# A three-block transformer forward pass: remainders of the weights on GpSimd, halves of k in another order in three stages, and another order for the queries of cross-attention

## What is computed

```python
for i in range(2):
    h = h + 0.5 * swiglu(rms_norm(h, ffa_norm[i]), ffa_w_gate_up[i], ffa_w_down[i])
    hn = rms_norm(h, mix_norm[i])
    h = h + (even_mixer(hn, ...) if i == 0 else odd_mixer(hn, ...))
    h = h + 0.5 * swiglu(rms_norm(h, ffb_norm[i]), ffb_w_gate_up[i], ffb_w_down[i])
    gate = sigmoid(rms_norm(h, ple_norm[i]) @ ple_w_gate[i])
    h = h + gate * (p[i] @ ple_w_proj[i])
x = rms_norm(h, final_norm)
proj = rmsnorm(x, norm_mix_g) @ w_in          # q, k, v, gelu inputs, two gates
x = x + (sigmoid(gate_a) * (moba(q, k, v) @ w_a) + sigmoid(gate_b) * (gmlp(u, v) @ w_b)) @ w_out
x = x + cross_attention(rmsnorm(x, norm_xa), rmsnorm(mem, norm_mem)) 
x = x + peer(rmsnorm(x, norm_ffn))            # top 16 of 128 x 128 keys per head, 8 heads
return rmsnorm(x, final_g)
```

## Time and profile before

| | |
|---|---|
| time, median of 3 runs | 2117.62 us (2116.42 to 2120.50) |
| the profiled execution's own time | 2120.12 us |
| its span in the trace | 2118.3 us |
| TensorE busy | 2091.8 us, 10466 matmuls |
| VectorE busy | 1338.4 us |
| ScalarE busy | 1049.0 us |
| GpSimd busy | 31.2 us, 42 instructions |
| remainders on VectorE (L267) | 336, 2290 ns each |
| w_hi on ScalarE (L262) | 336, 1915 ns each |
| mean granted TensorE clock | 0.997 |

### The profile page before, as it was taken

How to read it: one execution, slowest core, us unless ns; L and a number is a source line. 1 busy time by engine, 2 the same in 40 slices (tenths; PEclk the granted TensorE clock), 3 DMA queues, 4 the chain that set the end, 5 groups by cost and what they waited for, 6 DMA issues and landing times.

```text
span 2118.3 us, 25812 instructions
## 1 busy us (share of the span) xinstructions
PE 2091.8 (99%) x10466; PEld 1744.0 (82%) x10466; DVE 1338.4 (63%) x1793; ACT 1049.0 (50%) x1262; POOL 31.2 (1%) x42
## 2 busy tenths in 40 slices
PE   9999899999999999999999999999999999999998
PEld 7888788888888888888888878888888888888887
DVE  5445765456545566554675756799888656666665
ACT  5445564446444556444657555546455544444443
POOL 0100000000000000000100000000000000000000
PEclk9999999999999999999999999999999999999999
DMA  6654335554555442555554535577799997676772
GB/s 254 215 183 177 119 133 192 196 180 180 182 196 180 177 140 105 194 183 192 186 185 160 177 119 199 179 243 238 240 270 272 281 329 310 261 268 258 268 258 109
DMA packets 96596, 433.72 MB, mean 205 GB/s; under 512 B 7680, under 2 KB 41104, under 8 KB 51936
## 3 DMA queue, kind: packets, MB, share of 16 engines
q1 hardware_dynamic: 95152, 426.50, 57.2%
q0 software_dynamic: 1328, 5.58, 0.8%
HBM read 397.45 MB, written 34.60 MB: 204 GB/s over the span
## 4 chain that ended last, share of the span: by engine, by line
PE 94%; DVE 3%; ACT 1%; issue 1%; DMA 0%; POOL 0%; SPq 0%; POOLq 0%; DVEq 0%
PE bank L300 28%; PE bank L302 28%; PE bank L301 28%; PE bank L305 5%; PE bank L2224 2%; DVE w_lo L267 1%; PE bank L907 1%; PE bank L880 1%; PE bank L2057 0%; DMA h<-in_x 0%; DVE x_lo L336 0%; DVE arena L800 0%; ACT w_hi L262 0%; ACT arena L938 0%; ACT x_hi L327 0%
## 5 line engine op out<-in xcount | busy, mean ns | idle before, releaser
L267 DVE TENSOR_TENSOR w_lo<-raw,w_hi 128x2048 fp32r<-128x2048 f32 x336 | 768.7, 2290 | 510.0 <-ACT w_hi L262 509.9
L262 ACT ACTIVATE w_hi<-raw 128x2048 fp32r<-128x2048 f32 x336 | 643.0, 1915 | 721.2 <-PE bank L302 704.7
L300 PE MATMUL bank<-w_hi,x_hi 128*128 128x512 f32 (+1 forms) x2080 | 822.0, 395 | 4.6 <-DVE x_lo L336 3.3
L302 PE MATMUL bank<-w_hi,x_lo 128*128 128x512 f32 (+1 forms) x2080 | 810.1, 389 | 0.0
L301 PE MATMUL bank<-w_lo,x_hi 128*128 128x512 f32 (+1 forms) x2080 | 809.4, 389 | 0.0
L300 PEld LDWEIGHTS bank<-w_hi,x_hi 128*128 128x128 f32 x2080 | 391.5, 188 | 84.0 <-ACT gated L408 3.1
L302 PEld LDWEIGHTS bank<-w_hi,x_lo 128*128 128x128 f32 x2080 | 391.0, 188 | 82.1
L301 PEld LDWEIGHTS bank<-w_lo,x_hi 128*128 128x128 f32 x2080 | 391.7, 188 | 76.2
L300 PE MATMUL bank<-w_hi,a_hi 128*128 128x512 f32 x624 | 246.6, 395 | 0.2 <-DVE a_lo L995 0.2
L302 PE MATMUL bank<-w_hi,a_lo 128*128 128x512 f32 x624 | 243.2, 390 | 0.0
L301 PE MATMUL bank<-w_lo,a_hi 128*128 128x512 f32 x624 | 243.0, 389 | 0.0
(11 more groups left out here) (202 smaller groups left out, 1222.8 us busy)
## 6 DMA issues: line engine op xcount, KB each, us to landing
raw<-in_w SPq DMA_DIRECT2D x338, 1024.0 KB, 4.8
parked_t<-arena SPq DMA_DIRECT2D x32, 512.0 KB, 8.9
arena<-parked_t SPq DMA_DIRECT2D x8, 2048.0 KB, 9.4
arena<-parked_a SPq DMA_DIRECT2D x32, 512.0 KB, 5.8
parked_a<-one_i SPq DMA_DIRECT2D x21, 512.0 KB, 7.3
parked_a<-mid SPq DMA_DIRECT2D x11, 512.0 KB, 7.0
raw<-in_w SPq DMA_DIRECT2D x8, 256.0 KB, 6.3
one_i<-in_alibi POOLq DMA_DIRECT2D x1, 1024.0 KB, 5.2
```

The costliest lines, as they stand in the source:

```text
L262: act.activation(w_hi[:, u % RING, :, :], raw[:, u % RING, :, :], ACT.Copy).then_inc(*act_done.mark("w_hi", u))
L267: e.tensor_tensor(w_lo[:, u % RING, :, :], raw[:, u % RING, :, :], f32(w_hi[:, u % RING, :, :]), ALU.subtract).then_inc(*dve_done.mark("w_ ...
L300: pe.matmul(out, hi, w_hi[:, s, b, 0:width], start=start, stop=False)
L302: return pe.matmul(out, lo, w_hi[:, s, b, 0:width], start=False, stop=stop)
```

## The change

**GpSimd makes the remainders.** `lent` are the units from 8 on but for the two plain ones and nine `own` ones (ffa1 + 2 to + 5, units 85 to 88, and in2 + 2 to + 6, units 172 to 176). Their w_lo are made by GpSimd in the new `remainders`, called between its roots, clears and DMA issues; VectorE's `split_lo` skips them. `take` and `load_unit` wait for the engine that makes the remainder.

```diff
+        own = {u0 + i for u0, n in ((first["ffa1"] + LEAD, 4), (first["in2"] + LEAD, 5)) for i in range(n)}
+        lent = set(range(8, N_UNITS)) - set(plain) - own
+        def remainder_made(u):
+            return (pool_done if u in lent else dve_done)["w_lo", u]
...
-                sp.wait_ge(*dve_done["w_lo", u - RING])
+                sp.wait_ge(*remainder_made(u - RING))
...
+        def split_lo(dve, u):
+            if u < N_UNITS and u not in plain and u not in lent:
...
+        def remainders(pool, u0, u1):
+            for u in range(u0, u1):
+                if u in lent:
+                    pool.wait_ge(*act_done["w_hi", u])
+                    pool.tensor_tensor(w_lo[:, u % RING, :, :], raw[:, u % RING, :, :], f32(w_hi[:, u % RING, :, :]),
+                                       ALU.subtract).then_inc(*pool_done.mark("w_lo", u))
...
-            pe.wait_ge(*dve_done["w_lo", u])
+            pe.wait_ge(*remainder_made(u))
```

```diff
+        CROSSED = ("ffa1", "od_in", "in2")
+        for n in CROSSED:
+            u = first[n]
+            stored[u + 1], stored[u + 2] = u + 2, u + 1
...
+            tensor_up_half(pe, n, 0, 0, first[n], lambda: tensor_normed(pe, n, prev, 1), ready)
+            if n in CROSSED:
+                tensor_up_half(pe, n, 1, 0, first[n] + 1)
+                tensor_up_half(pe, n, 0, 1, first[n] + 2, None, ready)
+                tensor_up_half(pe, n, 1, 1, first[n] + 3)
+                tensor_back(pe, n, 0)
```

```diff
-            scalar_normed(act, "xa", 1, "xa", prev, XA_BANKS)
-            split_hi(act, q0 + LEAD)
-
-            act.activation(small[:, 80:81], gains[:, 0:1], ACT.Exp, scale=0.0)
+            scalar_normed(act, "xa", 1, "xa", prev, XA_BANKS,
+                          lambda: act.activation(small[:, 80:81], gains[:, 0:1], ACT.Exp, scale=0.0))
             act.wait_ge(*pe_done["block", "xq", 0, 0])
             scale_out(act, 0, bank[4][:, :], qn_x[:, 0, :]).then_inc(*act_done.mark("xq"))
+            split_hi(act, q0 + LEAD)
             split_hi(act, q0 + 1 + LEAD)
```

More of the change, by code:

```diff
@@ L262, in split_hi @@
                 act.activation(w_hi[:, u % RING, :, :], raw[:, u % RING, :, :], ACT.Copy).then_inc(*act_done.mark("w_hi", u))
[L264 to L268, removed]
+        def split_lo(dve, u):
+            if u < N_UNITS and u not in plain and u not in lent:
+                dve.wait_ge(*act_done["w_hi", u])
+                dve.tensor_tensor(w_lo[:, u % RING, :, :], raw[:, u % RING, :, :], f32(w_hi[:, u % RING, :, :]),
+                                  ALU.subtract).then_inc(*dve_done.mark("w_lo", u))
+        def remainders(pool, u0, u1):
[4 more added lines that the diff above has]
+                                       ALU.subtract).then_inc(*pool_done.mark("w_lo", u))
         def load_by_chunks(sp, u, meanwhile=None):
@@ L546, in ffn_down, with tensor_up_half @@
             return first[n] + (3 * c + 6 if c < NFC - 2 else 2 * NFC + c)
[L548 to L565, removed]
-                if i == 0 and meanwhile:
-                    meanwhile()
+        def tensor_up_half(pe, key, c, i, u, between=None, ready=None, free=None):
+            s = u if u < 2 else take(pe, u)
+            for t in range(NT):
+                if free:
+                    free(t)
+                if t == 1 and between:
+                    between()
+                for k in range(UB):
+                    kk = i * UB + k
+                    if ready and t == 0:
+                        ready(kk)
+                    last = product(pe, bank[gu(c)[t]][:, :], s, k, BLK, x_hi[:, kk, t * P:(t + 1) * P],
+                                   x_lo[:, kk, t * P:(t + 1) * P], kk == 0, kk == KC - 1)
+                last.then_inc(*pe_done.mark("unit", u, t))
+                if i == 1:
+                    pe_done.also("up", key, c, t)
+            pe_done.also("used", u)
         def tensor_down_half(pe, key, c, half):
@@ L671, in vector_ffn @@
                 vector_first_rest(dve)
-            split_lo(dve, ffn_up(n, 0) + 1 + LEAD)
-            both(0)
+            split_lo(dve, first[n] + 1 + LEAD)
+            if n not in CROSSED:
+                both(0)
             for c in range(1, NFC):
                 split_lo(dve, ffn_up(n, c) + LEAD)
+                if n in CROSSED and c == 1:
+                    both(0)
                 split_lo(dve, ffn_up(n, c) + 1 + LEAD)
@@ L1311, in tensor_odd @@
             unit(0)
+            unit(2)
             unit(1)
@@ L1833, in pool_moba @@
             pool.memset(values_m, 0.0).then_inc(*pool_done.mark("cleared", "moba"))
+            remainders(pool, first["ple_gate1"] + LEAD, first["in2"] + LEAD)
             pool_root(pool, "final1", 40)
             pool_root(pool, "mix2", 0)
+            remainders(pool, first["in2"] + LEAD, first["moba"] + LEAD)
             pool.wait_ge(*dve_done["o_lo", "M", 7])
@@ L1838, in pool_moba @@
             pool_root(pool, "v", 24)
+            remainders(pool, first["moba"] + LEAD, first["gmlp"] + LEAD)
             pool_root(pool, "mem", 32)
+            remainders(pool, first["gmlp"] + LEAD, first["xq"] + LEAD)
         kt_x, qn_x, qt_x = view(2048, HEADS_X, T), view(4096, NT, 512), view(5120, HEADS_X, T)
```

88 lines of the change are left out of this document (59 added, 29 removed).

## The result

The changed kernel takes 2191.54 us (median of 4 runs, 2190.76 to 2196.97) against 2117.07 us before: ratio 1.0354, 95% interval 1.0341 to 1.0367. It is 74.5 us slower where 6 us of gain were forecast, and lies outside the range of 2106 to 2139. The profiled execution has a span of 2189.0 us.

The account below looks back on a forecast made before the run. TensorE, busy 99%, was taken as the bound, only its waits winnable. 2120.1 (profiled) - 12.4 gains + 6.1 losses = 2113.8, or 2111.3 against the median of 2117.6; range 2106 to 2139, the forecast's own 2106 to 2116.

Parts of the forecast that it names:

- What bounds the kernel: TensorE is busy 99% of the span, so only its waits can be won, however many microseconds leave VectorE.
- The crossing: Halves of k crossed in ffa1, od_in and in2: x_lo waits go; with ev_in's, -3.9 us.
- What is late next: At ev_in, after the x_lo wait goes, GpSimd's rstd is late next, counted among the losses.
- Cross-attention: Table loaded under the rstd wait, queries scaled before the w_hi: TensorE's wait goes, -2.75 us, and lower clock, -1.7.
- The even mixer's 1.6 us: Removing the remainder at 234.31 from VectorE's row shortens TensorE's wait for scale L987 by 1.6 us (0 to 1.9).
- the wait of 0.98 at 272.04: Even mixer: a remainder at 268.22 stands ahead of the softmax that releases TensorE; removing it gives -1.1 us.
- The 3.5 us "at the lower level": Even mixer, 230 to 280: clock 0.93 read as 3.5 us at 1.2 GHz; taken as 0, kept for the range.
- GpSimd's 4.5 us: Length of one remainder on GpSimd, taken between two and three streams at the memset's rate.
- keeps up in dense stretches: GpSimd at 4.5 us a remainder fills 83% of a 5.4 us unit, so nothing is lost there.
- The series at the junctions: GpSimd's own work in series delays w_lo: ev_in +1.7 and +1.5, moba +2.6, even mixer's clears +0.3 us.
- Part 3: What GpSimd costs: losses only where its own work stands in series, 6.1 us in all.
- its first rival: GpSimd and VectorE hinder each other reading SBUF: table stage +25 us, routing +3, total 2136 (2122 to 2146); chance 0.29.

Follow-up runs that it names:

- e6: e1 with one unit lent, 41, whose w_lo stood inside the even mixer's unbroken row of VectorE work: 2110.28 us.
- e11: e1 with units 166, 167 and 168 lent, the series at the start of moba: 2115.86 us.
- e1: The changed kernel with no unit lent; crossed halves and ScalarE's new order in cross-attention stay: 2109.0 us.
- e8: The kernel before, plus three GpSimd memsets of 128x1024 that nobody waits for, for each of 25 table-stage units: 2116.48 us.
- e4: The changed kernel with only 152 units lent, all inside the four FFNs and the second half of PEER: 2113.09 us.
- e9: e1 with units 168, 169 and 170 lent, back to back behind two clears at the start of moba's preparation: 2118.49 us.

## Why the prediction was wrong, point by point

- **What bounds the kernel** was right: only TensorE's waits count. VectorE is busy 355 us less, and that was worth nothing as such. 321 remainders of 2.29 us are 735 us; that only 355 are missing puts, as an estimate, some 380 us of waiting for GpSimd into VectorE's records.
- **The crossing** was right in kind: the x_lo waits go in all three stages. The three were 3.4 of the 3.9 priced (ev_in is the rest) and brought 2.9: in od_in a w_hi is late next by the same 0.7 us. "What is late next" was asked of GpSimd's rstd only, and not of ScalarE.
- **Cross-attention** was right: -2.75 and -1.7 priced, -4.0 measured, with the clock whole.
- **The even mixer's 1.6 us** was wrong: the remainder at 234.31 stood ahead of VectorE's row, but the scale that TensorE waits for follows TensorE's own scores, and that wait did not shrink (e6). Nor did the wait of 0.98 at 272.04 go, priced at 1.1: in the changed kernel it is 3.67 us at 272.60, because the scale there waits for GpSimd's remainder that begins at 267.86. The 3.5 us "at the lower level" next to it is a slip: at half speed a mean of 0.93 over 50 us is 7 us at that level, which cost 3.5. It was no term of the sum.
- **GpSimd's 4.5 us** was right: 4.6 alone. That it keeps up in dense stretches was right too, to 0.05 us a stage.
- **The series at the junctions** were right in place and kind. At moba 2.6 was priced and 3.9 measured (e11), 0.8 of the excess from a remainder that waits for VectorE's; at ev_in 3.2 and 2.6. A third one of 3.0 us, at 746.37 in od_in, was not priced.
- **The step that failed** is the sentence of Part 3 that "nothing is lost except where GpSimd's own work stands in the row, in series". It puts at nothing what VectorE's operations lose beside GpSimd's remainders, and the losses in its sum come to 6.1 us. The runs show 82.5 us for the lending (changed kernel against e1), most of it VectorE's operations with two SBUF operands or from SBUF to SBUF that wait for a remainder, and TensorE behind them; the waits for remainders themselves, the only cost that the step knew, are 9.8 us of idle. The prediction knew of this as its first rival and gave it 0.29. The evidence against it was one row: two operations begun within 0.06 us of each other with no delay. It was an operation of two columns, and it says nothing on one of 2048: the changed kernel shows the same thing at 225.35 and 225.40, beside remainders that stretch whatever of this kind they meet. The prediction said that two elements say little and still gave the row weight. The Trainium skill, "SBUF — State Buffer", section "Who interferes with whom", states that VectorE and GpSimd share a pair of ports under an exclusive lock, held for a whole instruction; that an operation of VectorE with two SBUF inputs needs it against a GpSimd operation that reads SBUF, and not against one that only writes; and that copies and tensor_scalar from SBUF to SBUF need it in a two-port mode. The traces here agree on who waits: 84 of 116 such operations stretched (the rest stood in the two rows that held GpSimd up), 0 of more than 340 others, and no effect from memsets (e8).

```profile
225.35 0.69 POOL L440 TENSOR_TENSOR small<-small,consts_sb 128x2 f32<-128x2 f32 x1
...
225.40 0.19 DVE L1059 TENSOR_TENSOR arena<-arena,consts_sb 128x32 f32<-128x32 f32 x1
```

- **The rival's own size**, 25 us, was under a third of the truth. It priced the table stage at 25 less some lead (17 measured). It gave routing 3 (20 measured), because it summed busy time; routing ends in a serial chain in which every operation of 0.4 to 2.3 us can wait for a remainder. From L2188 to the end of the first four L2211 it takes 24.3 us in the changed kernel and 8.4 in e1, and L2211 releases TensorE after an idle of 8.2 us. And it left out all stages before PEER (43 us), since it looked only for places where VectorE is full, not for short operations with a waiting TensorE behind them. The four L2211 in e1, then in the changed kernel, beside three remainders:

```profile
1459.41 2.86 DVE L2211 TENSOR_TENSOR arena<-arena 128x2048 bf16<-128x2048 bf16 x4
...
1505.80 15.59 DVE L2211 TENSOR_TENSOR arena<-arena 128x2048 bf16<-128x2048 bf16 x4
...
1504.25 16.39 POOL L289 TENSOR_TENSOR w_lo<-raw,w_hi 128x2048 fp32r<-128x2048 f32 x3 [0.64 <-ACT w_hi L276]
```

## What to carry to other kernels

Before work goes from VectorE to GpSimd, list VectorE's operations that read two SBUF operands or scale from SBUF to SBUF, and see which of them TensorE waits for: each can be held up for a whole operation of GpSimd, here 4.6 us, and at one place for three in a row; the sum of busy times says nothing about that. A stretched operation costs only where something waits for it: the seven means of two columns took 2.5 us instead of 0.16, which cost 0.1 each, as their roots stood behind the same remainder. Where VectorE has one operand in PSUM or does reductions and searches, as in the FFNs here, GpSimd worked beside it at no cost (e4); it then pays only if VectorE was late there, and here it wasn't. Test a doubtful resource with work that nobody waits for, once reading and once only writing: two runs settled what no row of the kernel before could.

## What the runs showed of the hardware that I had not expected

How long a wait lasts. In e9 a 0.69 us add waits 10.85 us behind three remainders that stand back to back, and it works the other way too. In the changed kernel, GpSimd's remainder and VectorE in the table stage:

```profile
1623.60 19.65 POOL L289 TENSOR_TENSOR w_lo<-raw,w_hi 128x2048 fp32r<-128x2048 f32 x2 [4.83 <-ACT w_hi L276]
...
1638.19 10.07 POOL L289 TENSOR_TENSOR w_lo<-raw,w_hi 128x2048 fp32r<-128x2048 f32 x2
...
1621.65 0.68 DVE L2255 TENSOR_TENSOR arena<-iota_rep,arena 128x1024 bf16<-128x1024 bf16 x1
...
1631.88 1.89 DVE L2260 TENSOR_TENSOR arena<-arena 128x1024 bf16<-128x1024 bf16 x3
...
1637.29 1.50 DVE L2255 TENSOR_TENSOR arena<-iota_rep,arena 128x1024 bf16<-128x1024 bf16 x1 [3.52 <-PE bank L2270]
1638.71 5.09 DVE L2257 TENSOR_TENSOR arena<-iota_rep,arena 128x1024 bf16<-128x1024 bf16 x1
```

(The two rows of GpSimd are from two views; the second remainder of the first row is the first of the second.) The remainder of 1623.60 ends at 1638.23, 14.6 us later: an unbroken row of table operations, from 1621.65 to 1633.8, leaves it no gap, and its own 4.5 us begin only then. So a wait can last as long as the other engine's row.

It need not. At 1638.23 the next remainder's record has already begun, and still L2255, waiting since 1637.29, gets its turn and ends at 1638.79; L2257 behind it then waits for that next remainder. The remainder at 1656.82, shown above, began inside a row of VectorE's and had its turn after one operation. Counted over the changed kernel: where a remainder ended, another followed at once and an operation of VectorE stood waiting, nine had their turn there, and one, the add L805 of ple_gate1, had not, at two ends. Of the remainders that were held up while VectorE's row went on, 22 had their turn after one or two of its operations; the two that waited for the whole row waited for 17. The same add L805, at the end of ple_gate0, beside four remainders back to back:

```profile
506.15 19.32 POOL L289 TENSOR_TENSOR w_lo<-raw,w_hi 128x2048 fp32r<-128x2048 f32 x4 [2.03 <-ACT w_hi L276]
...
512.39 4.01 DVE L805 TENSOR_TENSOR h<-h,arena 128x512 f32<-128x512 f32 x1
```

It is done 0.6 us after the remainder that it met, with two more to come. What decides between the two cases no run here shows.

In ple_gate1 of the changed kernel a late series and a long wait meet:

```profile
1047.51 13.59 POOL L289 TENSOR_TENSOR w_lo<-raw,w_hi 128x2048 fp32r<-128x2048 f32 x3
...
1048.94 12.72 DVE L805 TENSOR_TENSOR h<-h,arena 128x512 f32<-128x512 f32 x1
...
1052.21 0.77 PE L322 MATMUL bank<-w_hi,x_hi 128*128 128x512 f32 x1 [3.05 <-POOL w_lo L289]
...
1063.04 1.33 PE L327 MATMUL bank<-consts_sb,h 128*128 128x128 f32 x5 [3.56 <-DVE h L805]
```

GpSimd comes to these remainders late, behind two others, the root and the clears, and then makes three in a row. TensorE idles 3.05 us for the first of them, runs at the lower clock after that stop (granted 0.57 over 1052 to 1056), and idles 3.56 us for the add L805, which takes 12.72 us: 10 us in a stage of 22.7.
